# Eight projection jobs, eight x jobs and k with the tokens on PSUM's partitions and the turning done by VectorE and DMAs

## What is computed

```python
u = rms_norm(h, mix_pre_g)
p_in, z, xbc, dt_raw, gates = split(u @ w_in)        # pooling | z | x,B,C | dt | gates
y_a = pool_mixer(p_in, pool_w, pool_scale) @ w_pool_out   # trailing means over 2, 4, 8, 16 tokens
xbc = silu(causal_depthwise_conv(xbc, conv_w, conv_b))    # four taps along the tokens
y = ssd_scan(x, softplus(dt), A, B, C) + d_skip * x       # 8 groups of 512 channels
y = rms_norm(y * silu(z)) per group
h = h + rms_norm((g_a * y_a + g_b * (y @ w_ssd_out)) @ w_mix_out)
k, v = mem_n @ w_k, mem_n @ w_v                           # cross-attention, q = u2 @ w_q
```

## Time and profile before

| | us |
|---|---|
| median of 3 runs (2731.93 to 2732.07) | 2731.94 |
| the profiled execution, its own time | 2732.21 |
| its span, first to last instruction | 2730.5 |
| PE busy | 2717.9 (100% of the span) |
| DVE busy | 1631.0 (60%) |
| ACT busy | 1289.9 (47%) |
| GpSimd busy | 345.9 (13%) |

### The profile page before, as it was taken

One profiled execution on the slowest core, in us unless ns is written; L12 is line 12 of the kernel. 1 busy time (PEld: TensorE's weight loads), 2 busy tenths in 40 slices (PEclk: granted clock), 3 DMA queues, 4 the chain that ended last, 5 costly groups with the idle time before them and its releaser, 6 DMA issues.

```text
span 2730.5 us, 39496 instructions
## 1 busy us (share of the span) xinstructions
PE 2717.9 (100%) x14076; PEld 2336.3 (86%) x14076; DVE 1631.0 (60%) x1920; ACT 1289.9 (47%) x1442; POOL 345.9 (13%) x619
## 2 busy tenths in 40 slices
PE   9999999999999999999999999999999999999998
PEld 7888888888899889989999888888988888888887
DVE  5555555544577556787887775566565555554444
ACT  5444444444454544455554564445654444444443
POOL 1121212000000000002122201223002122120000
PEclk9999999999999999999999999999999999999999
DMA  7777767666666665567667676668567677776664
GB/s 234 205 210 201 209 200 207 200 197 196 173 186 195 201 200 182 170 184 213 183 190 216 179 210 202 203 228 227 162 180 210 194 212 207 202 208 199 197 197 161
DMA packets 286770, 541.48 MB, mean 198 GB/s; under 512 B 27504, under 2 KB 28400, under 8 KB 286416
## 3 DMA queue, kind: packets, MB, share of 16 engines
q1 hardware_dynamic: 263520, 504.00, 60.7%
q0 software_dynamic: 22976, 36.07, 5.0%
q10 hardware_dynamic: 176, 0.07, 0.0%
HBM read 519.53 MB, written 2.16 MB: 191 GB/s over the span
## 4 chain that ended last, share of the span: by engine, by line
PE 98%; DVE 1%; DMA 0%; ACT 0%; issue 0%; DVEq 0%; ACTq 0%
PE J L660 26%; PE J L662 26%; PE J L661 26%; PE J L694 5%; PE J L697 5%; PE J L696 5%; PE J L737 1%; PE A L962 1%; PE A L963 1%; PE A L961 1%; PE J L733 0%; PE J L709 0%; DMA raw<-in_w_mix_out_dram 0%; PE J L674 0%; PE J L676 0%; PE J L675 0%
## 5 line engine op out<-in xcount | busy, mean ns | idle before, releaser
L1509 DVE TENSOR_TENSOR wl<-raw,wh 128x1024 fp32r<-128x1024 f32 x950 | 1154.5, 1222 | 961.8 <-ACT wh L1093 956.2
L1093 ACT ACTIVATE wh<-raw 128x1024 fp32r<-128x1024 f32 x950 | 1005.1, 1060 | 1305.2 <-PE J L662 1046.5
L660 PE MATMUL J<-wh,ul 128*128 128x512 f32 x2016 | 786.0, 390 | 2.3 <-DVE wl L1509 2.1
L662 PE MATMUL J<-wl,uh 128*128 128x512 f32 x2016 | 784.5, 389 | 0.0
L661 PE MATMUL J<-wh,uh 128*128 128x512 f32 x2016 | 784.4, 389 | 0.0
L660 PEld LDWEIGHTS J<-wh,ul 128*128 128x128 f32 x2016 | 378.6, 188 | 82.1 <-issue 4.0
L662 PEld LDWEIGHTS J<-wl,uh 128*128 128x128 f32 x2016 | 378.5, 188 | 79.0
L661 PEld LDWEIGHTS J<-wh,uh 128*128 128x128 f32 x2016 | 378.6, 188 | 77.5
L694 PE MATMUL J<-ul,wh 128*128 128x256 f32 x1056 | 300.2, 284 | 0.0
L697 PE MATMUL J<-uh,wl 128*128 128x256 f32 x1056 | 298.8, 283 | 0.0
L696 PE MATMUL J<-uh,wh 128*128 128x256 f32 x1056 | 298.8, 283 | 0.0
(11 more groups left out here) (293 smaller groups left out, 2262.4 us busy)
## 6 DMA issues: line engine op xcount, KB each, us to landing
raw<-in_ffn_w_dram SPq DMA_DIRECT2D x528, 512.0 KB, 4.3
raw<-in_w_in_dram SPq DMA_DIRECT2D x257, 512.0 KB, 3.9
raw<-in_w_ssd_out_dram SPq DMA_DIRECT2D x64, 512.0 KB, 3.6
raw<-in_w_pool_out_dram SPq DMA_DIRECT2D x32, 512.0 KB, 4.1
raw<-in_w_mix_out_dram SPq DMA_DIRECT2D x32, 512.0 KB, 6.2
hraw<-turned POOLq DMA_DIRECT2D x320, 32.0 KB, 4.0
csb<-cs_dram POOLq DMA_DIRECT2D x16, 512.0 KB, 7.4
raw<-in_pool_w_dram SPq DMA_DIRECT2D x8, 512.0 KB, 4.7
```

Source lines behind the costliest of these rows:

```text
L660: nc.tensor.matmul(o[:, t], b, wh[:, r, kk], start=(k == 0 and kk == 0), stop=False)
L662: mm = nc.tensor.matmul(o[:, t], a, wl[:, r, kk], start=False, stop=(k == last_k and kk == CK - 1))
L1093: nc.scalar.activation(wh[:, r], raw[:, r], ACT.Copy).then_inc(high, 1)
L1509: nc.vector.tensor_tensor(wl[:, r], raw[:, r], wh[:, r].bitcast(F32), ALU.subtract).then_inc(low, 1)
```

## The change

It does five things.

- The jobs pin0 to pin3, B0, C0, B1, C1, the eight x and k are made in token form: 8 x 17 = 136 chunks. ACT copies the result out of PSUM, for all but k times the token's factor (`tokens_out`), DVE turns blocks (`turn_tokens`), GpSimd issues the 16 DMAs (`move_tokens`), and DVE's windows or taps wait for these (`f_moved`). DVE's evacuations `pool_x` and `x_in`/`bc_in` are gone. The windows stand four chunks after the pw job's end, the taps of C0 five chunks after its end, of B1 in C1, of C1 in x of group 0, and those of x at the end of the z job.
- `turn_x` stands ahead of the third chunk of the next group's x job, `ssd` ahead of its sixth, the cb products two jobs later; in DVE's and ACT's queues the parts of a group are written in another order.
- At the start the second block of x is turned ahead of chunk 1, and one more advance stands ahead of the fourth block's norm on ACT and DVE.
- The memory's blocks are turned one at a time with an advance between.
- The loads of gate_a's and gate_b's rows wait for the moves, since `f_turn` lies on `row_bc`.

The diff, cut to its core:

```diff
+        bT = at("bT", 104, [P, M, S])
+        cT = at("cT", 108, [P, M, S])
+        b0_in = at("b0_in", 148, [P, M, S])
+        bc_in = at("bc_in", 112, [P, M, S])
+        f_raw = at("f_raw", 176, [P, T, NCOL])
+        f_turn = at("f_turn", 200, [P, M, M, T, 32])
...
+            def move_tokens(name, dst):
+
+                pool.wait_ge(f_turned, f_number(name) + 1)
+                move_natural(dst, f_turn, f_moved)
+
+            move_tokens("pin0", pool_x)
...
+            for g in range(1, 4):
+                move_tokens(f"pin{g}", pool_x)
...
+            move_tokens("B0", b0_in)
+            pool.wait_ge(f_moved, 256 * (f_number("B0") + 1))
...
+            for name in ("C0", "B1", "C1"):
+                move_tokens(name, bc_in)
...
+            for g in range(GROUPS):
+
+                if g < GROUPS - 1:
+                    pool.wait_ge(seg_ready, g + 1)
+                    load_csb(g + 1)
+                move_tokens(("x", g), x_in)
+                if g >= 1:
+                    move_y(g - 1)
+            pool.wait_ge(f_moved, 256 * len(TURNED_JOBS))
...
+            pool.wait_ge(k_turned, 1)
+            move_natural(kT, k_turn, k_moved)
...
-                        pass_chunk(("gate", f, 0), n, 1, X_FIRST, after_first=lambda: turn_res(n, (1,)))
+                        turn_res(n, (1,))
+                        pass_chunk(("gate", f, 0), n, 1, X_FIRST)
...
-            after_halves("pin0", 1, feature=True)
-            feature_chunks("pin0", uh, ul, range(4, 7), CD - 1, before=pre_wait(1))
+            after_halves("pin0", 1)
+            token_chunks("pin0", uh, ul, range(4, 7), CD - 1, before=pre_wait(1))
...
+            def token_job(name):
+                claim(name)
+                token_chunks(name, uh, ul, range(CD), CD - 1)
...
-            claim("B1")
-            feature_chunks("B1", uh, ul, range(0, 5), CD - 1)
+            token_job("B1")
+            claim("C1")
+            token_chunks("C1", uh, ul, range(0, 4), CD - 1)
             cb(0, 0)
-            feature_chunks("B1", uh, ul, range(5, 6), CD - 1)
+            token_chunks("C1", uh, ul, range(4, 5), CD - 1)
             cb(0, 1)
-            feature_chunks("B1", uh, ul, range(6, CD), CD - 1)
...
-                feature_chunks(("x", 0), uh, ul, range(0, 3), CD - 1, i, per)
+                token_chunks(("x", 0), uh, ul, range(0, 2), CD - 1, i, per)
+                if i is not None:
+                    turn_x(i)
+                token_chunks(("x", 0), uh, ul, range(2, 5), CD - 1, i, per)
+                if i is not None:
+                    ssd(i)
+                token_chunks(("x", 0), uh, ul, range(5, CD), CD - 1, i, per)
+                claim(("z", 0), i)
+                token_chunks(("z", 0), uh, ul, range(0, 4), CD - 1, i, per)
                 if i is None:
-                    feature_chunks(("x", 0), uh, ul, range(3, 5), CD - 1, i, per)
                     cb(1, 0)
-                    feature_chunks(("x", 0), uh, ul, range(5, 6), CD - 1, i, per)
+                token_chunks(("z", 0), uh, ul, range(4, 5), CD - 1, i, per)
+                if i is None:
                     cb(1, 1)
-                else:
...
-                token_chunks(("z", 0), uh, ul, range(0, 7), CD - 1, i, per)
-
-                pe.wait_ge(xc_silu, lin(1, i, 1))
-                claim_area(0, ("xT", 0), i, 1)
-                for t in range(T):
...
-            feature_chunks("k", memh, meml, range(0, 7), CD - 1)
+            token_chunks("k", memh, meml, range(0, 7), CD - 1)
...
+            pe.wait_ge(k_moved, 256)
...
+                if n == 0:
+                    advance()
                 pre_high(n, 3)
...
+            def tokens_out(name, dst, i=None, per=0):
+
+                n = f_number(name)
+                act.wait_ge(used, lin(end(name), i, per))
+                if n >= 1 or i is not None:
+                    act.wait_ge(f_turned, lin(n, i, 1))
+                for t in range(T):
+                    a = nc.scalar.activation(dst[:, t], tok(slot(name))[:, t], ACT.Copy, scale=sr_u[:, t:t + 1])
+                a.then_inc(evacuated[slot(name)], 1)
...
+            for g in range(3):
+                to(end(f"pin{g + 1}"))
+                tokens_out(f"pin{g + 1}", f_raw)
+                pool_mixed(g)
+                to(end(f"pw{g}") + 6 + g // 2)
+                pool_high(g + 1)
+            to(end("B0"))
+            tokens_out("B0", f_raw)
...
+            def x_copy(g0, i=None):
+
+                act.wait_ge(t_ready[0], lin(use(0, ("xT", g0)), i, 1))
+                nc.scalar.activation(X[:], A[:, 0], ACT.Copy).then_inc(t_moved[0], 1)
...
+                if i is not None:
+                    to(c0 + 1, i, per)
+                    conv_silu(("x", 0), xc[:], xc_silu, i - 1)
                     to(c0 + 3, i, per)
+                    x_copy(0, i - 1)
+                    to(c0 + 4, i, per)
                     finish_z(0, i - 1)
-                    to(c0 + 5, i, per)
+                    to(c0 + 7, i, per)
                     finish_square(0, i - 1)
-                    to(c0 + 6, i, per)
                     root(g_root + 1, i - 1)
                 to(c0 + CD, i, per)
+                tokens_out(("x", 0), zs, i, per)
+                to(c0 + CD + 1, i, per)
                 act.wait_ge(seg_ready, lin(1, i, 1))
                 nc.scalar.activation(E[:], E[:], ACT.Exp).then_inc(exp_ready, 1)
-                to(c0 + CD + 6, i, per)
-                conv_silu(("x", 0), xc[:], xc_silu, i)
...
             def pool_window(g):
-                done()
-                nc.vector.tensor_tensor(pool_x[:], feat(slot(f"pin{g}")), rbc[:].unsqueeze(1).to_broadcast([P, M, S]),
-                                        ALU.mult).then_inc(evacuated[slot(f"pin{g}")], 1)
-                dve.wait_ge(evacuated[slot(f"pin{g}")], moved(f"pin{g}"))
+                dve.wait_ge(f_moved, 256 * (f_number(f"pin{g}") + 1))
...
+            def turn_tokens(name, src, i=None):
+
                 dve.wait_ge(evacuated[slot(name)], lin(moved(name), i, 1))
+                turn_blocks(f_turn, src, f_turned)
...
+                dve.wait_ge(f_moved, lin(256 * (f_number(name) + 1), i, 256))
...
             to(end("pin0"))
+            turn_tokens("pin0", f_raw)
             dve.wait_ge(t_moved[0], use(0, "rbc"))
             dve.wait_ge(mix_loaded, 64)
-            pool_window(0)
...
+            to(end("dt") + 4)
+            pool_window(0)
+            to(end("dt") + 6)
             pool_low(0)
...
+            for g in range(3):
+                to(end(f"pin{g + 1}"))
+                turn_tokens(f"pin{g + 1}", f_raw)
+                if g == 0:
+                    dve.wait_ge(t_ready[1], use(1, "csT"))
+                    nc.vector.tensor_copy(cst[:], A[:, 1, 0, 0:P]).then_inc(t_moved[1], 1)
+                pool_mixed(g)
+                to(end(f"pw{g}") + 4)
+                pool_window(g + 1)
+                to(end(f"pw{g}") + 6 + g // 2)
+                pool_low(g + 1)
             to(end("B0"))
-            conv_in("B0")
+            turn_tokens("B0", f_raw)
...
+            conv_taps("C0", cT, INNER // P + GROUPS)
+            to(end("B1"))
+            turn_tokens("B1", f_raw)
...
+            dve.wait_ge(t_moved[1], use(1, ("cb", 1)))
+            conv_taps("B1", bT, INNER // P + M)
             to(end("C1"))
+            turn_tokens("C1", f_raw)
...
+                if i is not None:
+                    to(c0 + 1, i, per)
+                    weigh(slice(HPG // 2, HPG), 0, i - 1).then_inc(w_ready, 1)
+                    to(c0 + 3, i, per)
+                    scale_x(0, i - 1)
+                    to(c0 + 6, i, per)
+                    finish_gate(0, i - 1)
+                    to(c0 + 7, i, per)
...
+                if i is not None:
                     finish_var(0, i - 1)
+                else:
+                    to(c0 + 3)
+                subtract(range(HPG // 2, HPG)).then_inc(seg_ready, 1)
                 if i is None:
                     to(c0 + 5)
+                    conv_taps("C1", cT, INNER // P + GROUPS + M)
+                to(c0 + CD, i, per)
+                turn_tokens(("x", 0), zs, i)
+                if i is not None:
+                    to(c0 + CD + 1, i, per)
+                    finish_scale(0, i - 1)
+                to(c0 + CD + 4, i, per)
+                if i is None:
                     cb_masked(1, 0)
-                    to(c0 + 6)
-                    cb_masked(1, 1)
...
-                    if h == HPG // 2 - 1:
-                        to(c0 + 7, i, per)
-                l.then_inc(seg_ready, 1)
-                to(c0 + CD, i, per)
-                conv(("x", 0), xc, 0, i, per, M)
-                if i is not None:
-                    to(c0 + CD + 4, i, per)
-                    finish_scale(0, i - 1)
-                to(c0 + CD + 6, i, per)
-                if i is not None:
+                else:
                     dve.wait_ge(y_turned, i)
```

(36 more changed lines are left out.)

174 lines of the change are left out of this document (71 added, 103 removed).

## The result

The changed kernel takes 2742.8 us (median of 7 runs, 2738.99 to 2744.44) where the kernel before takes 2732.36 (7 runs, 2731.93 to 2732.55): a ratio of 1.0036, interval 1.0024 to 1.0047. It is slower, by 10 us, and the forecast was 2719.5. Its runs scatter by 5.5 us; those of before lie within 0.6 here, and within 3.7 in a later set of 27.

What follows compares the result with a forecast made beforehand. PE's matmul list and few stalls were taken to bound the kernel. Gains of 21.8 + 1.7 + 1.2 = 24.7 us against new waits of 1.6 + 2.7 + 8.0 = 12.3 gave 2719.5 us, range 2708 to 2732.

Steps and rivals of the forecast that it cites:

- What bounds, and the pace: PE holds 98% of the path; 136 chunks go from 2.88 to 2.72 us, 21.8 us less.
- rival D: Token chunks run at 2.88 us because something else paces them: 2741, or 2732 with waits hidden; chance 0.03.
- Start, memory, k: Waits at the start gone, 1.7 us; waits under the memory's turning gone, 1.2; k's move costs nothing.
- pin: In the pooling stage pw3 waits about 1.5 us for `pooll`, bounds 0.8 and 2.3; pin1 costs 0.1, pin2 nothing.
- B and C: C1's turn stands behind B1's taps, so z of group 0 waits for its split: 2.7 us, bounds 0 and 4.
- The price of a move: From first x DMA to taps 13.4 us, 13.7 from the turn's end; 1.0 us of wait a group, 8.0 in all.
- Rival B: x moves issued right behind csb's 1 MB load land 1.5 us later, in eight groups: 2727 to 2737; chance 0.17.
- The counter-argument: Against late x moves: csb's load lands at 37 in the group, x's last DMA is issued only at 41.7.
- rival C: x's move shares rings with csb, landing in 7.4 us, not 4.0: 2747; tellably slower from 2.2 us a move; chance 0.08.
- The size of a late landing: In the groups, lateness of x's move goes straight into PE's wait: 1.5 us late in eight groups costs 12 us.

Runs made afterwards that it cites:

- e2: The changed kernel without the 128 DMAs that move x, the taps reading `uh` instead: 2713.41 us, ratio 0.9933.
- e1: The kernel before with only the earlier turn of x's second block, the extra split and the memory blocks turned one at a time: 2728.41 us, ratio 0.9985.
- e5: The changed kernel with GpSimd issuing x's move first and waiting for its landing before the csb load and y's move: 2741.64 us, ratio 1.0037.
- e4: The changed kernel with GpSimd waiting for x's landing before it issues the move of y: 2740.14 us, ratio 1.0027.
- e3: The changed kernel with the move of x issued ahead of the next group's csb load: 2736.19 us, ratio 1.001.
- e6: The changed kernel with x's taps one split later on VectorE, x's turning and the scan one chunk later on TensorE: 2724.88 us, ratio 0.9975.
- e13: e2 with six copies on VectorE ahead of the taps in each group, to make PE stall without a DMA: 2753.16 us.
- e7: The changed kernel with the edits of e3 and e6 together: 2718.73 us, ratio 0.995.
- e8: e7 with pin1's move ahead of the store of the decay rows and pin3's low window part one split earlier: 2717.98 us, ratio 0.9947.
- e11: e7 with csb ahead of x in the first group alone and pin1's move ahead of the store of the decay rows: 2719.32 us, ratio 0.9955.

## Why the prediction was wrong

**What bounds, and the pace: right.** Matmuls of 512 columns start 0.2267 us apart in the x jobs, rival D is out, and in e2, with the group waits gone, the profiled span is 20.6 us shorter than before: 132 chunks of 0.16 and 3.3 at the start and the memory, less 2.8 of waits for `pooll` and about 1 in small pieces.

**Start, memory, k: right.** -1.6 and -1.7 for 1.7 and 1.2 predicted; e1 has them alone, 3.9. k's move starts at 1933.31 and PE asks for it at 1957.50, without a wait.

**pin: half right.** pw3 waits 1.41 us for 1.5 predicted. pw1 waits 1.69 for 0.1: pin1's move begins only at 796.69, behind the store of the decay rows and 3.38 us of waiting for its landing. The step named that store and gave it no price. That is 1.5 of the stretch's 2.5 us. The rest is in small pieces: the four chunks of pin0's that go through the norm's passes gave 0.3 us in place of 0.6, and each wait has 0.16 us around it.

**B and C: too high.** 0.64 us for 2.7, mainly since C1's move took 11.6 us and not 13.4. That this came out low was luck, and it hid 2 us of what the groups lost.

**The price of a move, the step that failed.** It took 13.4 us from two y moves that had 12.65 and 14.11 and set the upper end at 14.11 and 0.3 from the turn. The lags of x are 15.3 to 15.6 in six of the eight groups, 2.1 over. Of this 1.3 us go where csb and the y move are both kept off (e5), and 0.4 where y alone is (e4), so most of it is csb directly ahead; e3 and the last group show the same. Rival B, and not the forecast, had the mechanism; its lag was 1.5 us over, rival C's 3.4. The counter-argument, that csb lands before the last DMA of x is issued, held to the letter (in the group above csb had landed at 1266.64, and that DMA was issued at 1267.95), but the DMA took 6.2 us for all that; why the delay outlasts csb's landing is open. The rest is that even alone in its queue the move has a lag of 14.0 to 14.4 (e5), 0.6 to 1.0 over the value taken.

**The size of a late landing, the second failure.** Everything ahead of the landing was well laid out: the turn began 31.1 us behind the x job's start, half pace taken off, for 30.9 predicted. From the landing on, a stall of 2.8 us follows by the prediction's own sum from a lag of 15.5. But all cases priced it one to one. Behind a stall of 2.7 us PE's clock falls to half and 1.56 us more is lost, so a lag 2.1 us over the forecast cost 3.7 a group, and the period of a group is 54.4 to 54.7 us where 50.8 was forecast. The forecast with six groups at 3.7 more and the last at 1.0 more is 2742.7. That this is the measured time to 0.1 is luck, since pin (2.5 over), B and C (2.1 under) and the 3 us around the stalls are not in it. As an estimate from the stalls above, the change becomes slower by more than can be told where half pace sets in, about 1.3 us of lag over the forecast, not 2.2. Rival C's 2747 is near, but by a landing of 7.4 us, where the median for x was 6.0. Half pace was nowhere in the chances, so the range ended 11 us short.

## What to carry to other kernels

A transfer that takes the place of an evacuation needs its lag read behind the same neighbours in its queue; the same kind of DMA elsewhere in the trace gives a hint and no more: here it was 2 us short. A stall of PE over some 2 us is to be priced with the half pace that may stand behind it, here 1.6 us each. And what stands behind the wait in the waiting engine's queue can decide more than the lag: e6 took 18 us off without touching the move, half of it by keeping the stalls below the length at which half pace comes.

## What the runs showed of the hardware

- PE at half pace behind a stall: rows 0.427 apart for about 3 us, 1.5 to 1.7 us lost (2.7 and 2.9 in two cases, behind stalls of 3.3), always from 2.7 us of stall on (14 of 14), sometimes from 1.87. That it makes the runs scatter is not shown: the changed kernel's differ by 5.5 us, but so do those of e6 (6.0), whose profile has no half pace, and e13's, with seven stretches of it, by only 1.2.
- 16 DMAs of 32 KB from GpSimd's queue take 0.58 us an issue, 9.2 to 9.7 in all, and the last lands 11.6 to 14.4 us after the first was issued (pin, C0, B1, C1 and k in the changed kernel; x where csb is behind, in most groups). Right behind two loads of 512 KB the landing of one has a median of 6.0 us in place of 4.0, and the last lands at 15.0 to 15.3. By the formula in the Trainium skill, "DMA: Bandwidth & Descriptors", section "Anatomy of one DMA — SWDGE (gpsimd) path", one takes an estimated 2.1 us. The quickest of x's 128 come near it (1.8 us in e3, 2.2 in the changed kernel), the medians do not.
- GpSimd pauses in the middle of a row of equal DMAs: for 5.5 to 6.2 us in the first group's move of x, after the twelfth, where no csb load is ahead of it (e3, e5, e7, e8), and for 6.5 to 7.2 us in B0's, after the fourth, directly behind a csb load, in the changed kernel and every run made from it but e8 and e11. So a csb load ahead is not what prevents it. B0's move, 20.2 us from first DMA to landing in the changed kernel, has a job and more of cover, so it cost nothing there. What GpSimd does in the pause no row shows.
- Four operations on VectorE took 1.90 us instead of 1.38 where GpSimd began to issue the csb load within 0.02 us of their start (six groups of e5), and 1.39 where it began y's DMAs (e5's last group).
